# Two transformer layers on one core: a modulation matrix laid out for sums along the free dimension, splits of whole pairs of weight rows, and buffers at multiples of 64 bytes

## What is computed

```python
silu_c = jax.nn.silu(c)
mod = silu_c @ w_ada[l] + b_ada[l]
shift_m, scale_m, gate_m, shift_f, scale_f, gate_f = jnp.split(mod, N_MOD, axis=-1)
h = modulate(rmsnorm(x, g_norm_mix[l]), shift_m, scale_m)      # h * (1 + scale) + shift
proj = h @ w_in[l]
# two kinds of attention on proj, eight heads each, giving o_diff and o_mla
mix = jnp.concatenate([o_diff, o_mla], axis=-1) @ w_out[l]
x = x + gate_m[:, None, :] * mix
h = modulate(rmsnorm(x, g_norm_ffn[l]), shift_f, scale_f)
f = jnp.square(jax.nn.relu(h @ w_ff1[l])) @ w_ff2[l]
x = x + gate_f[:, None, :] * f
```

## Time and profile before

| | |
|---|---|
| median of 3 runs | 2256.26 us |
| lowest and highest run | 2246.44 and 2257.49 us |
| profiled execution, first to last instruction (span) | 2249.4 us |
| TensorE matmul busy | 2028.9 us (90%) |
| VectorE busy | 1452.0 us (65%) |
| ScalarE busy | 1061.2 us (47%) |
| GpSimd busy | 215.8 us (10%) |
| moved by DMA | 450.01 MB, mean 200 GB/s |
| mean granted TensorE clock | 0.958 |

### The profile page before, as it was taken

One profiled execution on the slowest core, in us unless ns is written; L12 is line 12 of the kernel. 1 busy time (PEld: TensorE's weight loads), 2 busy tenths in 40 slices (PEclk: granted clock), 3 DMA queues, 4 the chain that ended last, 5 costly groups with the idle time before them and its releaser, 6 DMA issues. The chain is left out here.

```text
span 2249.4 us, 26960 instructions
## 1 busy us (share of the span) xinstructions
PE 2028.9 (90%) x9432; PEld 1673.3 (74%) x9432; DVE 1452.0 (65%) x2623; ACT 1061.2 (47%) x2120; POOL 215.8 (10%) x247
## 2 busy tenths in 40 slices
PE   5568868977869899999999999988999999999999
PEld 4456656755657688888888887977988887888877
DVE  6887787767778765555555555667666655556544
ACT  3444434553454444544544554545545454444443
POOL 0020043300100010011011012020001001001000
PEclk9788988987999999999999999998999999999999
DMA  8779877636868856555556555643554456666654
GB/s 301 239 248 295 284 262 251 229 94 220 281 234 297 270 178 199 182 189 186 188 173 202 183 181 191 195 117 106 152 148 144 121 162 200 182 196 186 189 188 158
DMA packets 239209, 450.01 MB, mean 200 GB/s; under 512 B 14304, under 2 KB 45280, under 8 KB 238432
## 3 DMA queue, kind: packets, MB, share of 16 engines
q1 hardware_dynamic: 236096, 435.84, 60.5%
q0 software_dynamic: 1856, 9.44, 1.2%
q10 hardware_dynamic: 1120, 3.01, 0.4%
HBM read 444.03 MB, written 4.19 MB: 199 GB/s over the span
## 5 line engine op out<-in xcount | busy, mean ns | idle before, releaser
L235 DVE TENSOR_TENSOR wlo<-raw,whi 128x512 fp32r<-128x512 f32 (+4 forms) x1336 | 896.2, 705 | 516.8 <-ACT whi L234 491.8
L234 ACT ACTIVATE whi<-raw 128x512 fp32r<-128x512 f32 (+4 forms) x1336 | 772.9, 605 | 779.0 <-PE g L326 470.8
L324 PE MATMUL g<-whi,lhsA_hi 128*128 128x512 f32 (+4 forms) x1840 | 716.3, 389 | 43.4 <-DVE wlo L235 34.3
L326 PE MATMUL g<-whi,lhsA_lo 128*128 128x512 f32 (+4 forms) x1840 | 695.0, 378 | 0.0
L325 PE MATMUL g<-wlo,lhsA_hi 128*128 128x512 f32 (+4 forms) x1840 | 694.5, 377 | 0.0
L324 PEld LDWEIGHTS g<-whi,lhsA_hi 128*128 128x128 f32 x1840 | 353.7, 192 | 116.2 <-DVE wlo L235 49.8
L326 PEld LDWEIGHTS g<-whi,lhsA_lo 128*128 128x128 f32 x1840 | 352.3, 191 | 56.9
L325 PEld LDWEIGHTS g<-wlo,lhsA_hi 128*128 128x128 f32 x1840 | 353.7, 192 | 52.4 <-issue 1.2
L493 DVE SCALAR_TENSOR_TENSOR acc<-raw,small,acc 128x512 f32<-128x512 f32 x360 | 278.7, 774 | 37.6 <-DMA raw<-in_w_ada 14.6
L324 PE MATMUL g<-whi,lhsF_hi 128*128 128x512 f32 x512 | 203.8, 398 | 1.1 <-DVE wlo L235 1.1
L325 PE MATMUL g<-wlo,lhsF_hi 128*128 128x512 f32 x512 | 202.2, 395 | 0.0
(11 more groups left out here) (291 smaller groups left out, 1690.2 us busy)
## 6 DMA issues: line engine op xcount, KB each, us to landing
raw<-in_w_ff SPq DMA_DIRECT2D x256, 512.0 KB, 4.3
raw<-in_w_ada SPq DMA_DIRECT2D x192, 512.0 KB, 4.8
raw<-in_w_in SPq DMA_DIRECT2D x176, 512.0 KB, 4.4
raw<-in_w_out SPq DMA_DIRECT2D x64, 512.0 KB, 4.7
raw<-in_w_in SPq DMA_DIRECT2D x80, 384.0 KB, 3.6
raw<-in_w_mem_kv SPq DMA_DIRECT2D x16, 512.0 KB, 5.4
raw<-in_w_branch_a SPq DMA_DIRECT2D x12, 512.0 KB, 4.1
raw<-in_w_branch_b SPq DMA_DIRECT2D x12, 512.0 KB, 3.9
```

What stands on the lines that cost most here:

```text
L234: t_hi = AC.put(lambda e, x=x, hi=hi: e.activation(hi, x, ACT.Copy), landed[j], free)
L235: t_lo = DV.put(lambda e, x=x, hi=hi, lo=lo: e.tensor_tensor(lo, x, hi.bitcast(F32), ALU.subtract), landed[j], t_hi, free)
L324: PE.put(lambda e, o=o, x=xh, w=h, f=first: e.matmul(o, x, w, start=f, stop=False), w, mark=False)
L326: tok = PE.put(lambda e, o=o, x=xl, w=h, f=last: e.matmul(o, x, w, start=False, stop=f), mark=t == 1)
```

## The change

1. **Layout.** The host transposes `w_ada` (`across`): partition p of chunk part (m, h) holds output column 128 m + p with 1024 of its 2048 inputs, contiguous. A pair of `w_ada` is now 128 x 1024 with one run of 4 KB for each partition in place of two of 2 KB.
2. **Sums.** `silu(c)` is spread over all partitions (`srow`, 128 x 2048), by one more load at the head of ACT's queue, one Tanh and one VectorE instruction. `ada_part` is one VectorE instruction for a pair, 128 x 1024, that multiplies and gives the sum of its products (`accum_out`) into one of eight columns (`halfsums`). The `acc` buffers, the ScalarE instruction of each chunk and the matmuls of line 517 go. `ada_reduce` adds the two half sums and the bias on VectorE. For a gate it then makes four diagonal blocks (128 x 128) on VectorE and multiplies them by ones on TensorE, and VectorE copies the result. The gates' bias comes with `vec` (32 columns more); the two POOL loads go.
3. **Wide splits.** A weight pair is split by one ScalarE and one VectorE instruction of 2 n columns, into `NSPLIT = 3` buffers of 1024. `run` first issues the eight matmuls of a pair that need only `hi`, which wait for ScalarE's part alone, and then the four with `lo`.
4. **Alignment.** `cst` has 1328 columns (5312 bytes, 83 x 64) for 1320 (5280, 82.5 x 64), and `vec` lies in 208 (832, 13 x 64) for 173 (692 bytes), so that what is allocated behind them starts at a multiple of 64 bytes.

```diff
-NRAW, NSPLIT = 4, 7
+NRAW, NSPLIT = 4, 3
...
-    whi = sb("whi", [P, NSPLIT, 512], F32R)
-    wlo = sb("wlo", [P, NSPLIT, 512], F32R)
+    whi = sb("whi", [P, NSPLIT, 1024], F32R)
+    wlo = sb("wlo", [P, NSPLIT, 1024], F32R)
...
-    vec = sb("vec", [P, V_END])
+    vec = sb("vec", [P, 208])[:, 0:V_END]
...
-        plan.append((kind, a["w_ada"][0, k0 * P:(k0 + 2) * P, 512 * c:512 * c + 512], 512, (c, k0)))
+        plan.append((kind, a["w_ada"][4 * c + k0 // 4, k0 // 2 % 2], 512, (c, k0)))
...
-            parts = []
-            for kk in range(2):
-                s = state["nsplit"]
-                state["nsplit"] += 1
-                free = read[s - NSPLIT] if s >= NSPLIT else []
-                x, hi, lo = src[:, kk * n:kk * n + n], whi[:, s % NSPLIT, 0:n], wlo[:, s % NSPLIT, 0:n]
-                t_hi = AC.put(lambda e, x=x, hi=hi: e.activation(hi, x, ACT.Copy), landed[j], free)
-                t_lo = DV.put(lambda e, x=x, hi=hi, lo=lo: e.tensor_tensor(lo, x, hi.bitcast(F32), ALU.subtract),
-                              landed[j], t_hi, free)
-                parts.append((s, hi, lo, t_lo))
-            halves[j] = parts
+            s = state["nsplit"]
+            state["nsplit"] += 1
+            free = read[s - NSPLIT] if s >= NSPLIT else []
+            hi, lo = whi[:, s % NSPLIT, 0:2 * n], wlo[:, s % NSPLIT, 0:2 * n]
+            t_hi = AC.put(lambda e: e.activation(hi, src, ACT.Copy), landed[j], free)
+            t_lo = DV.put(lambda e: e.tensor_tensor(lo, src, hi.bitcast(F32), ALU.subtract), landed[j], t_hi, free)
+            halves[j] = (s, hi, lo, t_hi, t_lo)
...
+        sv = srow[:, D // 2 * (i % 2):D // 2 * (i % 2) + D // 2]
+        b.tok = DV.put(lambda e: e.scalar_tensor_tensor(
+            out=src, in0=src, scalar=0.5, in1=sv, op0=ALU.mult, op1=ALU.mult, accum_out=b.ap[:, i:i + 1]),
+            t_in, ready_c["silu"], b.free)
...
+            t = DV.put(lambda e: e.tensor_tensor(col, pr[:, :, 0], pr[:, :, 1], ALU.add), b.tok)
+            t = DV.put(lambda e: e.tensor_tensor(col, col, bias, ALU.add), t, ready_c["vec"])
+            dg = take(tmps)
+            for m in range(4):
+                t = DV.put(lambda e, m=m: e.tensor_scalar(dg.ap[:, P * m:P * m + P], ident, col[:, m:m + 1], None, ALU.mult),
+                           t, dg.free, t_cst)
+            T = take(TB)
+            tok = PE.put(lambda e: e.matmul(T.ap[:, :], ones, dg.ap[:, :], start=True, stop=True), t, T.free)
...
+def across(w):
+    return np.ascontiguousarray(w.T.reshape(6 * D // P, P, 2, D // 2).transpose(0, 2, 1, 3))
```

More of the change, by code:

```diff
@@ L216, in load_to @@
             kind, src, n, _ = plan[j]
-            dst = raw[:, j % NRAW, 0:2 * n].rearrange("p (k n) -> p k n", k=2)
-            landed[j] = SP.dma(dst, src.rearrange("(k p) n -> p k n", p=P), raw_sem[j % NRAW], raw_free[j % NRAW])
+            dst = raw[:, j % NRAW, 0:2 * n]
+            if kind == "w":
+                dst, src = dst.rearrange("p (k n) -> p k n", k=2), src.rearrange("(k p) n -> p k n", p=P)
+            landed[j] = SP.dma(dst, src, raw_sem[j % NRAW], raw_free[j % NRAW])
             state["load"] += 1
@@ L313, in run @@
                 pump(1, 3)
-            for kk in range(2):
-                k = 2 * i + kk
-                ka = 2 * pair + kk
-                s, h, l, t_lo = halves[j][kk]
-                for t in range(2):
-                    o = G[2 * par + t][:, 0:n]
-                    xh = lhs.hi[:, ka, t * P:t * P + P]
-                    xl = lhs.lo[:, ka, t * P:t * P + P]
-                    first, last = k == 0, k == K - 1
-                    w = [t_lo, lhs.ready[pair]] + (gfree[par] if first else [])
-                    PE.put(lambda e, o=o, x=xh, w=h, f=first: e.matmul(o, x, w, start=f, stop=False), w, mark=False)
-                    PE.put(lambda e, o=o, x=xh, w=l: e.matmul(o, x, w, start=False, stop=False), mark=False)
-                    tok = PE.put(lambda e, o=o, x=xl, w=h, f=last: e.matmul(o, x, w, start=False, stop=f),
-                                 mark=t == 1)
-                read[s] = [tok]
+            s, hi, lo, t_hi, t_lo = halves[j]
+            steps_of = [(kk, t) for kk in range(2) for t in range(2)]
+            end = i == len(u["tiles"]) - 1
+            for kk, t in steps_of:
+                o, h = G[2 * par + t][:, 0:n], hi[:, kk * n:kk * n + n]
+                xh = lhs.hi[:, 2 * pair + kk, t * P:t * P + P]
+                xl = lhs.lo[:, 2 * pair + kk, t * P:t * P + P]
+                first = i == 0 and kk == 0
+                w = [t_hi, lhs.ready[pair]] + (gfree[par] if first else [])
+                PE.put(lambda e, o=o, x=xh, w=h, f=first: e.matmul(o, x, w, start=f, stop=False), w, mark=False)
+                PE.put(lambda e, o=o, x=xl, w=h: e.matmul(o, x, w, start=False, stop=False), mark=False)
+            for kk, t in steps_of:
+                o, l = G[2 * par + t][:, 0:n], lo[:, kk * n:kk * n + n]
+                xh = lhs.hi[:, 2 * pair + kk, t * P:t * P + P]
+                tok = PE.put(lambda e, o=o, x=xh, w=l, f=end and kk == 1: e.matmul(o, x, w, start=False, stop=f), t_lo,
+                             mark=kk == t == 1)
+            read[s] = [tok]
             pump(steps, width)
@@ L503, in ada_token @@
         return ada_done[c]
[L505 removed]
+    gate_free = {}
     def ada_reduce(c, b):
[L509 removed]
+        pr = b.ap.rearrange("p (m h) -> p m h", h=2)
         if c // 4 in (2, 5):
             j = c % 4
[L512 removed]
+            col = gcols[:, 4 * j:4 * j + 4]
+            bias = vec[:, V_BG + 16 * (c // 4 == 5) + 4 * j:][:, 0:4]
+            t = DV.put(lambda e: e.tensor_tensor(col, pr[:, :, 0], pr[:, :, 1], ALU.add), b.tok)
[6 more added lines that the diff above has]
+            tok = PE.put(lambda e: e.matmul(T.ap[:, :], ones, dg.ap[:, :], start=True, stop=True), t, T.free)
+            dg.release([tok])
             dst = gt[:, 512 * j:512 * j + 512]
[L514 to L518 removed]
+            ada_done[c] = DV.put(lambda e: e.tensor_copy(dst, T.ap[:, :]), tok, gate_free[c // 4])
+            T.release([ada_done[c]])
+        else:
             sec = {0: 0, 1: 1, 3: 2, 4: 3}[c // 4]
@@ L548, in build @@
     k = ready_c["vec"] = t_cols
-    cc = vec[:, V_C:V_C + 16]
-    ec = sm(16)
-    k1 = AC.put(lambda e: e.activation(ec, cc, ACT.Tanh, scale=0.5), k)
-    k1 = DV.put(lambda e: e.scalar_tensor_tensor(out=ec, in0=ec, scalar=1.0, in1=cc, op0=ALU.add, op1=ALU.mult), k1)
-    ready_c["silu"] = DV.put(lambda e: e.tensor_scalar(silu, ec, 0.5, None, ALU.mult), k1)
+    half = region[:, 4096:6144]
+    k1 = AC.put(lambda e: e.activation(half, srow[:, :], ACT.Tanh, scale=0.5), t_c)
+    ready_c["silu"] = DV.put(lambda e: e.scalar_tensor_tensor(out=srow[:, :], in0=half, scalar=1.0, in1=srow[:, :],
+                                                              op0=ALU.add, op1=ALU.mult), k1)
     k = DV.put(lambda e: e.tensor_scalar(vec[:, V_SUB:V_SUB + 1], vec[:, V_SUB:V_SUB + 1], 1.0 - LAM0, None,
@@ L1650 @@
     given = {n: np.ascontiguousarray(inputs[n]) for n in NAMES}
+    given["w_ada"] = across(inputs["w_ada"][0])
     given["const_tile"] = const_tile()
```

59 lines of the change are left out of this document (22 added, 37 removed).

## The result

| | before | after |
|---|---|---|
| median of four runs | 2253.49 us | **2287.79 us** |
| range | 2246.44 to 2257.49 | 2276.88 to 2292.52 |
| profiled span | 2249.4 | 2287.0 |
| mean granted clock of TensorE | 0.958 | 0.948 |

The changed kernel is slower: ratio 1.0143, 95% interval 1.0116 to 1.017, some 32 us. The forecast was 2206, 50 us faster, with 2262 as the high end of its range. It was wrong in sign.

What follows compares the result with a forecast made beforehand. Up to 770 us no single bound, behind it TensorE. The terms, -13 -15 -12 +2.5 +3 -15 -3 +3, sum to -49.5, say -50 us: 2256 - 50 = 2206 us, range 2140 to 2262.

Steps and rivals of the forecast that it cites:

- DMA runs of 4 KB: Early part: modulation pairs load faster in 4 KB runs, 0.2 us a pair for 67 pairs: -13 us (0 to -17).
- line 517: Early part: its matmuls go, with 37.5 us of PE waiting, a third counted: -12 us (0 to -37).
- longer start: Kernel start: the row of `c`, its load, Tanh and product come before the first sum: +2.5 us.
- gates: Early part: each of eight gates adds VectorE instructions and a copy waiting for a matmul: +3 us (0 to +16).
- 64 bytes: TensorE: stationary buffers at multiples of 64 bytes save 6.6 ns on each of 2304 matmuls: -15 us (0 to -15).
- splits: VectorE's relief, early and late: Weight pairs: splits 0.14 us shorter, 22 us of VectorE before 770 us; in the late part worth -3 us.
- What bounds the kernel now: Up to 770 us no single bound, 270 us of it close to the DMA queue's limit; behind it TensorE.
- The two signs: PE idle behind 800 us past 60 us, or the new VectorE instruction over 2 us, would mean forecast wrong.
- VectorE in the early part: Up to 770 us: sums (1.42 us an instruction) and splits save 47 us of VectorE: -15 us (0 to -31).
- Late part: Order and depth in the TensorE bound part: -3 us from VectorE's relief, +3 us from the shallower split ring.
- The ring rival: Between 1350 and 1800 us: the split ring is too short, +51 us, 2256 us, no change; chance 0.12.
- Half pace: Early part: the sum halves VectorE's pace, 2.5 us an instruction, 2300 us, slower; chance 0.15.

Runs made afterwards that it cites:

- e3: The changed kernel with the splits put back to 512 columns in six halves, matmuls in the old order; new sums, layout, alignment stay: 2255.79 us, ratio to before 1.0001.
- e4: The kernel before with a split ring of six halves in place of seven, nothing else: 2254.31 us, ratio 0.9995.
- e2: The kernel before with pair wide splits, a ring of three pairs and the new matmul order: 2280.45 us, ratio 1.0112.
- e6: The kernel before with 512 wide splits in six halves, new matmul order, both halves given back at the pair's end: 2258.69 us, ratio 1.0014.

## Why the prediction was wrong

The terms against what the runs bound (differences of ratios, us; the measured ones add up to the 32 within 1):

| term | forecast | measured |
|---|---|---|
| DMA runs of 4 KB, VectorE's shorter sums, line 517, longer start | some -30 | -6, all four |
| gates | +3 | +12 with narrow splits (16 with wide ones; the 4 are among the 7 left over) |
| 64 bytes | -15 | -5 |
| splits: VectorE's relief, early and late | some -10 | width +22 |
| ring depth | +3 | order and release +3, depth 0 |
| left over, sums and splits together | | +7 |

The -6 is worked out: e3 lies 1.4 over e4, of which -5 are the alignment and +12 the gates. The gates' figure is what the late matmul gives back, so they may cost more, and the four terms of the -6 may have gained more.

*What bounds the kernel now* is the step that failed. It read the DMA share of 0.87 as "close to what the queue delivers", and priced the rest by the time that VectorE is busy. The bound was neither: it was four buffers, each turning in 7.1 us, of which 4.7 are the transfer and 2 the holding, and a fifth buffer alone was worth 46 us. By VectorE's busy time the wide split saves 0.14 us a pair, and the prediction counted it as a gain of some 10 us; it holds a buffer 0.36 us longer, and it cost 22. The sentence "in the other 500 us the raw buffers turn too slowly" was the right reading, held for the 270 us too, and was then priced by VectorE's busy time. By the traces (e2 less e6) some 14 of the 22 us fall before 820 us, and that they come about through the ring is argued, not shown, as said above. The two signs by which the prediction would have called itself wrong did not appear: the new instruction takes 1.32 us and not over 2, and behind 790 us PE idles 51 us and not over 60. They watched the instruction and the late part, and most of the loss is in neither.

*DMA runs of 4 KB.* The rate rose little: between 20 and 750 us a 4 KB packet of the changed kernel takes 194 ns on its engine in the mean where a 2 KB one takes 100, 3% less a byte. The median landing of a modulation pair is 4.6 us, 4.8 before; of that 0.2 a ring of four passes on a quarter. The 388 GB/s of the earlier trace rows came from the start, where the ACT queue fills beside SP's.

*VectorE in the early part.* The instruction's length was right, 1.32 us for 1.42. The sums do hold a buffer shorter, some 1.3 against 1.55 us, and with narrow splits (e3) they bring a lead of 10 us at 200 us and 11 at 463. The wide splits take it back: the changed kernel has 8 and 2.

*Line 517.* Gone, but the prediction did not name what is late next: the first half unit of `w_in` needs `x`, PE waits 14.9 us for POOL to scale it, and the lead of 15 us at 112 is 3.4 at 146.

*Start.* +3.7 us for 2.5 on the memory rows; the first sum starts at 13.62 us where 10.7 was worked out.

*Gates.* Priced by the length of the new instructions; the cost is their place in a queue of VectorE that runs pairs ahead of TensorE. The sum was off besides: half of 1.1 + 1 us is 1.05 and not 0.4 us, and eight times that is +8, still short of what was measured.

*Late part.* Forecast 0 in all, 11 us were lost. In the changed kernel 5.4 of them lie in the three units above; in e2 those are waits 0.6 to 0.9 us longer, each with a drop of the clock behind it. The rest was not traced. The ring rival had the place and missed the mechanism: from seven halves to six nothing of the depth is seen.

*Half pace.* The Trainium skill's "Vector Engine (DVE) Microarchitecture Reference", section "Points that are easy to get wrong", was the ground of this rival. Its rule, half the throughput for this kind of instruction with two SBUF sources that are not bf16, does not hold here even with the sum, if the pace of the subtract is taken as the full one: 1024 columns take a median of 1218 ns, as the subtract's 1226 do.

## What to carry to other kernels

A ring of few buffers is a loop of transfer and use, and it can set the pace while the DMA share reads 0.87. The queue's waits for a released buffer don't tell the two apart, as they stand with five buffers as well; one more buffer, or transfers of half the size, do. An instruction that makes two engines work one after the other on a whole tile instead of overlapped on halves saves busy time and holds the buffer longer. A wait that a change removes may have hidden another: the 9.7 us at line 517 came back as 14.9 for `x`. And where one engine looks ahead, a small result that another engine needs now stands behind all of it: put the reader later, or take the input from what has long been done.

## What the hardware showed unasked

POOL's multiply of 128x384 takes 1098 ns in the mean beside subtracts of 384 columns on VectorE and 1447 beside subtracts of 768, with the same operands, and the subtract beside it takes 0.63 us longer than alone. The 512 wide adds of line 1113 go from 1444 to 1609; those with nothing on VectorE beside them take 1252 to 1280 in both kernels, the longest 1757 beside 512 columns and 2287 beside 1024. Work moved to POOL is not free for VectorE, and a wider instruction on one costs the other.

Reading the accumulator costs 82 ns on VectorE, 190 on ScalarE.

The matmuls on `lhsF`, `yz` and `lhsY` stay 4.5 ns longer than those on `lhsA` at full clock with all buffers at multiples of 64 bytes.
